# A transformer pair's setup stage: input issued first, parameters on another queue, more slots for the modulation rows, square sums between the turns

## The chip, the cores and the metric

The kernel runs on one core of one Trainium2 chip. The metric is the device time of one execution in microseconds, lower being better: 2711.04 us is the median of 3 runs (2708.45 to 2712.81).

## What is computed

Two transformer blocks in float32 on a sequence of 1024 tokens and 1024 channels. Only the very beginning matters here: a conditioning vector `c` gives six modulation vectors, and the first of them shift and scale the normalised input before the first projection.

```python
def first_block(x, c, w_ada, b_ada, pre_mix_g, w_in, ...):
    c_act = jax.nn.silu(c)
    for l in range(DEPTH):
        mod = c_act @ w_ada[l] + b_ada[l]
        sh1, sc1, g1, sh2, sc2, g2 = [t[:, None, :] for t in jnp.split(mod, N_MOD, axis=-1)]
        h = rms_norm(x, pre_mix_g[l]) * (1.0 + sc1) + sh1
        y = token_mixer(h, w_in[l], ...)
        x = x + g1 * rms_norm(y, post_mix_g[l])
        h = rms_norm(x, pre_ffn_g[l]) * (1.0 + sc2) + sh2
        y = conv_ffn(h, w_up[l], ffn_conv_w[l], ffn_conv_b[l], w_down[l])
        x = x + g2 * rms_norm(y, post_ffn_g[l])
    return x
```

A second block (attention beside a pooling mixer, then a gated feed-forward part) follows; the change does not touch it.

## The kernel before

The activations are kept transposed (128 partitions of channels by 1024 tokens, eight such tiles). Every projection multiplies a weight tile of 1024 by 128, loaded by SyncE (SP) into one of two `raw` buffers, split by ScalarE (`split_hi`, L210) and VectorE (`split_lo`, L215) into a high and a low part, and used by TensorE in three products for each of eight channel tiles and two token halves (`product`, L259). Tile w+2 can be loaded only when tile w has been split (`load`, L197). The kernel is a row of blocks (`nc.Block`), and no engine begins a block before all have ended the one ahead of it.

Block "setup" (L437 to L587), engine by engine, each in its written order:

- GpSimd fills constants (identity, ones, masks). Its first memset, of `par_in`, is what SP waits for.
- SP issues 16 small parameter transfers (L480), `x` in two halves of 2 MB (L484), four rows of the modulation weights `w_ada` (512 KB each, one for each of four slots in `cbuf`, L486), seven very small transfers (L490 to L496), weight tiles 0 and 1 (L204), then twelve more `w_ada` rows, each when its slot has been read, the gate columns (L506), and tiles 2 and 3, which wait until tiles 0 and 1 are split.
- TensorE turns the parameters (L516), then `x`: eight turns of eight 128 by 128 transposes (L523) into two PSUM tiles used in turn; then the sums of squares (`sum_squares`, L368, 16 matmuls of 128x512, each two instructions); then, twice, it sums the accumulator of the modulation rows over the partitions (`reduce_ada`, L374).
- ScalarE makes the sigmoid of `c` (L540), copies the eight turned tiles to `xt` (L543), squares all eight into `squares`, which lies on the space of the input rows `xin` (L547), makes two constants, and splits tiles 0 and 1.
- VectorE copies the parameters (L561), waits for all seven very small transfers and scales the sinks (L563), makes `csil` (L567), adds eight modulation rows (L424, L425), waits for the reduction, makes `mod` (L429), zeroes the gate buffer (L579), adds eight more rows into the same accumulator, waits again, and then splits tiles 0 and 1 (L215) and the gate columns (L586).

Block "w_in" (L745) begins with the normalisation (`Norm.act`, L626: a table load, Ln, Exp, then eight `hhi` tiles; `Norm.dve`, L659: eight scaled tiles and eight `hlo` tiles) on ScalarE and VectorE, and with `pair_products` (L378) on TensorE, which multiplies tiles 0 and 1 as the `hlo` tiles come. Ahead of the normalisation both engines split tiles 2 and 3 (L809 and L905). SP parks `x` in DRAM (L618) and loads two rope tables.

Of the kernel before, what the change touches and what calls it, by code (L numbers as in the profile page):

```python
# [114 lines left out]
def block_kernel(nc, a, out):  # L115
    ctx = ExitStack()
    with ctx:
# [40 lines left out]
        hhi = sb("hhi", [P, DK, T], F32R)  # L158
        hlo = sb("hlo", [P, DK, T], F32R)
# [241 lines left out]
        ada_acc = ar(64, D)  # L401
# [4 lines left out]
        s_par, s_x, s_small = sem("params_loaded"), sem("x_loaded"), sem("small_loaded")  # L406
        s_ada = [sem(f"ada_loaded{i}") for i in range(4)]
# [3 lines left out]
        squares, x_sums = ar(32, DK, T), up[0][:, :]  # L411
# [25 lines left out]
        with nc.Block("setup") as block:  # L437
# [31 lines left out]
            @block.sync  # L469
            def _(sp):  # L470
                sp.wait_ge(s_pool, 1)
                srcs = {"ffn_conv_w01": a["ffn_conv_w"][0, 0:2, :].rearrange("t (j p) -> (t j) p", p=P),
                        "ffn_conv_w2": a["ffn_conv_w"][0, 2:3, :].rearrange("t (j p) -> (t j) p", p=P),
                        "ml_conv_w": a["ml_conv_w"][0].rearrange("t (j p) -> (t j) p", p=P),
                        "ml_norm_g": a["ml_norm_g"][0], "pool_b_2": a["pool_b_2"][0]}
                r = 0
                for name, k in PAR_ROWS:
                    if not name.startswith("pad"):
                        src = srcs[name] if name in srcs else a[name].rearrange("a (j p) -> (a j) p", p=P)
                        sp.dma_start(par_in[r % P:r % P + k, r // P, :], src).then_inc(s_par, 16)  # L480
                    r += k
                xv = a["x"][0].rearrange("(b p) d -> p b d", p=P)
                for b in range(2):
                    sp.dma_start(xin[:, 4 * b:4 * b + 4, :], xv[:, 4 * b:4 * b + 4, :]).then_inc(s_x, 16)  # L484
                def ada_load(slot, seg, k):
                    sp.dma_start(cbuf[:, slot, :], ada_rows(seg, k)).then_inc(s_ada[slot], 16)  # L486

                for k in range(4):
                    ada_load(k, 0, k)
                sp.dma_start(sinks_in, a["attn_sinks"].partition_broadcast(P)[:, 0, :]).then_inc(s_small, 16)  # L490
                for b in range(2):
                    for col, name in ((16, "q_norm_g_2"), (17, "k_norm_g_2")):
                        sp.dma_start(small[64 * b:64 * b + 64, col:col + 1], a[name].rearrange("a p -> p a"))\
                          .then_inc(s_small, 16)
                sp.dma_start(small[0:4, 18:19], a["ml_i_b"].rearrange("a p -> p a")).then_inc(s_small, 16)
                sp.dma_start(small[32:36, 18:19], a["ml_f_b"].rearrange("a p -> p a")).then_inc(s_small, 16)  # L496
                for w in range(RAW):
                    load(sp, At(w), tile_source(At(w)))

                for n in range(4, ADA_FIRST * DK):  # L500
                    sp.wait_ge(ada_added, n - 3)
                    ada_load(n % 4, n // DK, n % DK)
                sp.wait_ge(gate_zero, 1)
                for g in range(2):
                    src = a["w_in"][0].rearrange("(k p) c -> p k c", p=P)[:, :, GATE_COL + 4 * g:GATE_COL + 4 * g + 4]
                    sp.dma_start(gateF[:, :, 32 * g:32 * g + 4], src).then_inc(gate_loaded, 16)  # L506
                for w in range(RAW, 4):
                    load(sp, At(w), tile_source(At(w)))

            @block.tensor  # L510
            def _(pe):
# [6 lines left out]
                pe.wait_ge(s_x, 32)  # L518
                for k in range(DK):
                    if k >= 2:  # L520
                        pe.wait_ge(x_copied, k - 1)
                    for b in range(NB):
                        mm = nc.tensor.transpose(down[k % 2][:, b * P:(b + 1) * P], xin[:, b, k * P:(k + 1) * P],  # L523
                                                 identF[:, :])
                    mm.then_inc(x_turned, 1)

                pe.wait_ge(par_copied, 1)
                for k in range(DK):
                    pe.wait_ge(x_squared, k + 1)
                    sum_squares(x_sums, squares[:, k, :], k == 0, k == DK - 1)  # L530
                for s in range(ADA_FIRST):
                    pe.wait_ge(ada_added, s * DK + DK)
                    reduce_ada(up[1], 0, ada_acc).then_inc(ada_reduced, 1)

            @block.scalar
            def _(act):
                act.sem_inc(hi_done, RAW)
# [3 lines left out]
                for k in range(DK):  # L541
                    act.wait_ge(x_turned, k + 1)
                    nc.scalar.activation(xt[:, k, :], down[k % 2][:, :], ACT.Copy).then_inc(x_copied, 1)  # L543

                for k in range(DK):
                    act.wait_ge(x_copied, k + 1)
                    nc.scalar.activation(squares[:, k, :], xt[:, k, :], ACT.Square).then_inc(x_squared, 1)  # L547
# [3 lines left out]
                nc.scalar.activation(bandR[:, :, :], band, ACT.Copy).then_inc(consts, 1)  # L551
                for w in range(AHEAD):
                    split_hi(act, At(w))
# [4 lines left out]
            def _(dve):  # L558
# [3 lines left out]
                dve.wait_ge(s_small, 16 * 7)  # L562
                nc.vector.tensor_scalar(sinks, sinks_in, 1.0 / SC, None, ALU.mult).then_inc(sinks_scaled, 1)  # L563
# [3 lines left out]
                ch.link(nc.vector.tensor_tensor(csil, csig, par_col("c", 0, 8), ALU.mult))  # L567

                for s in range(ADA_FIRST):
                    for k in range(DK):  # L570
                        dve.wait_ge(s_ada[k % 4], s * 32 + 16 * (k // 4 + 1))
                        if s + k:
                            dve.wait_ge(ada_added, s * DK + k)
                        add_ada_row(ada_acc, cbuf[:, k % 4, :], k).then_inc(ada_added, 1)
                    dve.wait_ge(ada_reduced, s + 1)
                    ch.link(modulate(s, up[1][:, 0:DK]))
                    if s == 0:
                        dve.wait_ge(consts, 3)
                        nc.vector.memset(gateF[:, :, :], 0.0).then_inc(gate_zero, 1)  # L579
# [3 lines left out]
                for w in range(AHEAD):  # L583
                    split_lo(dve, At(w))
# [160 lines left out]
        with nc.Block("w_in") as block:  # L745
# [111 lines left out]
            def _(dve):  # L857
# [46 lines left out]

                for t in range(2):  # L905
                    split_lo(dve, At(t + AHEAD))
                norm_mix.dve(dve)
# [1485 lines left out]
```

## Time and profile before

| what | value |
|---|---|
| median of 3 runs | 2711.04 us (2708.45 to 2712.81) |
| profiled execution, its own time | 2708.46 us |
| its span | 2706.7 us |
| mean granted TensorE clock | 0.957 of full |
| TensorE matmul busy | 2446.0 us (90%) |
| VectorE busy | 1301.5 us (48%) |
| ScalarE busy | 840.2 us (31%) |
| first product matmul of block "w_in" | starts at 83.35 us |

Times in the profile count from the start of the span. A row of a timeline gives start, duration, engine, line, operation, the names it writes and reads, how many instructions are merged, and in brackets the idle time before it and what ended that. A start less the end of the row before it is idle time; a row with x2 holds two instructions back to back.

### The profile page before, as it was taken

Reading aid. Unit: us, or ns where it says so; the run is one execution under the profiler, and the core shown is the slowest. Engines: PE = TensorE matmul, PEld = TensorE weight load, DVE = VectorE, ACT = ScalarE, POOL = GpSimd, SP = SyncE. Lnnn points to the kernel's source line nnn. Section 1 sums busy time; section 2 is a strip of 40 time slices with the busy share of each in tenths; the row PEclk is TensorE's granted clock in tenths of the full one; section 3 lists DMA queues with packets and bytes.
Section 4 is the critical chain, followed back from the end, with each engine's and each line's share of the span. In section 5 each row is a group of like instructions: output and inputs, shape, how many; then the busy total and the mean of one; then the engine's idle time right before and its main releaser. Section 6 shows DMA issues by size and latency. Waiting matters only on the chain. (4 is left out here: it accounts for less than half of the span.)

```text
span 2706.7 us, 28720 instructions
## 1 busy us (share of the span) xinstructions
PE 2446.0 (90%) x10911; PEld 1971.0 (73%) x10911; DVE 1301.5 (48%) x1542; ACT 840.2 (31%) x1200; POOL 275.3 (10%) x206
## 2 busy tenths in 40 slices
PE   4799974569799999999997997898989999999998
PEld 3578864548488888888884865776778888888887
DVE  3467346751744444444446337996343333333333
ACT  3322134642432222222224346875131111111111
POOL 1000011312000000000002424552100000000000
PEclk8899997789899999999998998999999999999999
DMA  5335521002211111111113110002111111111111
GB/s 205 117 109 158 185 72 61 0 24 101 78 47 47 47 46 49 53 53 46 46 46 146 61 32 1 0 0 78 47 39 48 54 46 46 46 46 54 47 46 70
DMA packets 170071, 169.25 MB, mean 63 GB/s; under 512 B 7229, under 2 KB 153485, under 8 KB 169105
## 3 DMA queue, kind: packets, MB, share of 16 engines
q1 hardware_dynamic: 168529, 163.05, 18.6%
q0 software_dynamic: 1472, 5.26, 0.5%
q8 instruction: 45, 0.74, 0.1%
q14 instruction: 25, 0.20, 0.0%
HBM read 146.26 MB, written 22.04 MB: 62 GB/s over the span
## 5 line engine op out<-in xcount | busy, mean ns | idle before, releaser
L267 PE MATMUL ps<-hhi,whi 128*128 128x512 f32 x1984 | 776.2, 391 | 3.4 <-DVE cbuf L1953 2.7
L269 PE MATMUL ps<-hhi,wlo 128*128 128x512 f32 x1984 | 772.0, 389 | 0.0
L268 PE MATMUL ps<-hlo,whi 128*128 128x512 f32 x1984 | 771.9, 389 | 0.0
L215 DVE TENSOR_TENSOR wlo<-raw,whi 128x1024 fp32r<-128x1024 f32 x180 | 231.5, 1289 | 455.0 <-ACT whi L210 454.9
L267 PEld LDWEIGHTS ps<-hhi,whi 128*128 128x128 f32 x1984 | 372.4, 188 | 83.8 <-DVE cbuf L1953 3.1
L268 PEld LDWEIGHTS ps<-hlo,whi 128*128 128x128 f32 x1984 | 372.4, 188 | 78.8 <-issue 1.9
L269 PEld LDWEIGHTS ps<-hhi,wlo 128*128 128x128 f32 x1984 | 372.4, 188 | 77.7
L210 ACT ACTIVATE whi<-raw 128x1024 fp32r<-128x1024 f32 x180 | 186.3, 1049 | 429.4 <-PE ps L1868 299.9
L1985 DVE TENSOR_TENSOR arena<-arena,ps 128x1024 f32<-128x1024 f32 x176 | 214.7, 1220 | 155.6 <-PE ps L1868 154.5
L1866 PE MATMUL ps<-hid_hi,whi 128*128 128x512 f32 x704 | 275.2, 391 | 0.0
L1867 PE MATMUL ps<-hid_lo,whi 128*128 128x512 f32 x704 | 274.1, 389 | 0.0
L1868 PE MATMUL ps<-hid_hi,wlo 128*128 128x512 f32 x704 | 273.9, 389 | 0.0
L1493 POOL TENSOR_TENSOR cbuf<-cbuf,attn_stats 128x1024 f32<-128x1024 f32 x80 | 151.5, 1894 | 216.1 <-DVE attn_stats L1619 216.1
L1949 DVE SCALAR_TENSOR_TENSOR cbuf<-ps,par,cbuf 128x1023 f32<-128x1023 f32 x44 | 56.4, 1283 | 235.7 <-ACT cbuf L1893 235.6
L1866 PEld LDWEIGHTS ps<-hid_hi,whi 128*128 128x128 f32 x704 | 132.1, 188 | 31.4 <-DVE arena L1985 4.1
L1868 PEld LDWEIGHTS ps<-hid_hi,wlo 128*128 128x128 f32 x704 | 132.1, 188 | 27.7
L1867 PEld LDWEIGHTS ps<-hid_lo,whi 128*128 128x128 f32 x704 | 132.1, 188 | 27.1
L1749 POOL TENSOR_TENSOR cbuf<-cbuf 128x1024 f32<-128x1024 f32 x18 | 43.1, 2394 | 936.8 <-ACT cbuf L1739 936.8
L1893 ACT ACTIVATE cbuf<-ps,par 128x1024 f32<-128x1024 f32 x44 | 53.1, 1206 | 240.9 <-PE ps L269 232.3
L392 PE MATMUL ps<-hhi,whi 128*128 128x512 f32 x192 | 80.7, 420 | 45.8 <-DVE hlo L690 23.5
L1539 PE MATMUL ps<-identF,cbuf 128*128 128x128 f32 x640 | 93.9, 292 | 21.0 <-POOL cbuf L1493 15.7
L1907 ACT ACTIVATE hid_hi<-cbuf 128x1024 fp32r<-128x1024 f32 x44 | 46.5, 1058 | 211.0 <-DVEq L1964 115.6
(277 smaller groups left out, 2704.4 us busy)
## 6 DMA issues: line engine op xcount, KB each, us to landing
raw<-in_w_up SPq DMA_DIRECT2D x66, 512.0 KB, 3.6
raw<-in_w_down SPq DMA_DIRECT2D x44, 512.0 KB, 3.5
raw<-in_w_in SPq DMA_DIRECT2D x32, 512.0 KB, 5.9
arena<-in_w_ada SPq DMA_DIRECT2D x32, 512.0 KB, 5.1
x_park<-arena SPq DMA_DIRECT2D x3, 4096.0 KB, 12.3
raw<-in_w_gate SPq DMA_DIRECT2D x22, 512.0 KB, 3.6
cbuf<-in_w_ada SPq DMA_DIRECT2D x16, 512.0 KB, 5.3
raw<-in_w_out SPq DMA_DIRECT2D x16, 512.0 KB, 3.3
```

The source lines that it names most:

```text
L210: nc.scalar.activation(whi[:, w.off % RING, :], raw[:, w.off % RAW, :], ACT.Copy).then_inc(hi_done, 1)
L215: nc.vector.tensor_tensor(wlo[:, w.off % RING, :], raw[:, w.off % RAW, :], whi[:, w.off % RING, :].bitcast(F32), ALU.subtract).then_inc(lo ...
L267: nc.tensor.matmul(acc[:, tok], whi[:, s, ws], hhi[:, k, tok], start=(k == 0), stop=False)
L268: nc.tensor.matmul(acc[:, tok], whi[:, s, ws], hlo[:, k, tok], start=False, stop=False)
L269: mm = nc.tensor.matmul(acc[:, tok], wlo[:, s, ws], hhi[:, k, tok], start=False, stop=(k == DK - 1))
L392: nc.tensor.matmul(o, whi[:, s, ws], hhi[:, k, tok], start=(k == 0), stop=False)
L1493: nc.gpsimd.tensor_tensor(p, p, st[:, sl, 16:16 + q].unsqueeze(2).to_broadcast([P, q, T // q]), ALU.mult).then_inc(S["scaled"], 1)
L1539: mm = nc.tensor.transpose(ps_t[:, (4 * h + k) * P:(4 * h + k + 1) * P], src, identF[:, :])
L1866: nc.tensor.matmul(o, whi[:, s, ws], hidhi[:, p, tok], start=(r == 0), stop=False)
L1867: nc.tensor.matmul(o, whi[:, s, ws], hidlo[:, p, tok], start=False, stop=False)
L1868: mm = nc.tensor.matmul(o, wlo[:, s, ws], hidhi[:, p, tok], start=False, stop=(r == 1))
L1985: nc.vector.tensor_tensor(y[:, fo, :], y[:, fo, :], down[fo % 2][:, :], ALU.add)\
```

## The change

In SP's program `x` comes first and no longer waits for GpSimd; then eleven `w_ada` rows at once (four slots in `cbuf`, seven in `chunk_work`, which is the space of `hhi`), tiles 0 and 1, the gate columns, the last five `w_ada` rows, tiles 2 and 3. The 16 parameter transfers and the seven very small ones are issued by ScalarE. TensorE takes a sum of squares between two turns, starts a turn of the first half of `x` before the second is there, and reduces the first accumulator after the fifth sum. The second set of rows has its own accumulator and its own PSUM columns. ScalarE squares each tile right after its copy, into `lead_work` (the space of `hlo`). VectorE no longer waits for the small transfers before `csil`, zeroes the gate buffer first, adds all 16 rows with one `mod` step after the thirteenth, and splits tiles 0 and 1 before the second `mod` step. In block "w_in" the normalisation comes ahead of the splits of tiles 2 and 3.

```diff
@@ block "setup", SP
-                sp.wait_ge(s_pool, 1)
+                xv = a["x"][0].rearrange("(b p) d -> p b d", p=P)
+                for b in range(2):
+                    sp.dma_start(xin[:, 4 * b:4 * b + 4, :], xv[:, 4 * b:4 * b + 4, :]).then_inc(s_x[b], 16)
+                for n in range(len(ada_slots)):
+                    ada_load(n)
+                for w in range(RAW):
+                    load(sp, At(w), tile_source(At(w)))
+                sp.wait_ge(gate_zero, 1)
+                for g in range(2):
...
+                    sp.dma_start(gateF[:, :, 32 * g:32 * g + 4], src).then_inc(gate_loaded, 16)
+                for n in range(len(ada_slots), ADA_FIRST * DK):
+                    sp.wait_ge(ada_added, n - len(ada_slots) + 1)
+                    ada_load(n)
+                for w in range(RAW, 4):
+                    load(sp, At(w), tile_source(At(w)))
@@ block "setup", TensorE
+                turn(0)
+                turn(1)
+                pe.wait_ge(par_copied, 1)
+                for k in range(DK):
+                    if k + 2 < DK:
+                        turn(k + 2)
+                    sums(k)
+                    if k == 4:
+                        pe.wait_ge(ada_added, DK)
+                        reduce_ada(up[1], 0, ada_acc[0]).then_inc(ada_reduced, 1)
+                pe.wait_ge(ada_added, 2 * DK)
+                reduce_ada(up[1], HALF, ada_acc[1]).then_inc(ada_reduced, 1)
@@ block "setup", ScalarE
+                act.wait_ge(s_pool, 1)
...
+                        act.dma_start(par_in[r % P:r % P + k, r // P, :], src).then_inc(s_par, 16)
                 nc.scalar.activation(csig, par_col("c", 0, 8), ACT.Sigmoid).then_inc(c_sig, 1)
                 nc.scalar.activation(identR[:, :], identF[:, :], ACT.Copy).then_inc(consts, 1)
                 nc.scalar.activation(bandR[:, :, :], band, ACT.Copy).then_inc(consts, 1)
+                act.dma_start(sinks_in, a["attn_sinks"].partition_broadcast(P)[:, 0, :]).then_inc(s_small, 16)
...
+                for k in range(DK):
+                    act.wait_ge(x_turned, k + 1)
+                    nc.scalar.activation(xt[:, k, :], down[k % 2][:, :], ACT.Copy).then_inc(x_copied, 1)
+                    act.wait_ge(x_copied, k + 1)
+                    nc.scalar.activation(squares[:, k, :], xt[:, k, :], ACT.Square).then_inc(x_squared, 1)
@@ block "setup", VectorE
-                dve.wait_ge(s_small, 16 * 7)
-                nc.vector.tensor_scalar(sinks, sinks_in, 1.0 / SC, None, ALU.mult).then_inc(sinks_scaled, 1)
+                dve.wait_ge(consts, 3)
+                nc.vector.memset(gateF[:, :, :], 0.0).then_inc(gate_zero, 1)
+                for n in range(ADA_FIRST * DK):
+                    slot, k = n % len(ada_slots), n % DK
+                    dve.wait_ge(s_ada[slot], 16 * (n // len(ada_slots) + 1))
...
+                    if n == 12:
+                        dve.wait_ge(ada_reduced, 1)
+                        ch.link(modulate(0, up[1][:, 0:DK]))
+                for w in range(AHEAD):
+                    split_lo(dve, At(w))
+                dve.wait_ge(ada_reduced, 2)
+                ch.link(modulate(1, up[1][:, HALF:HALF + DK]))
@@ block "w_in", ScalarE (VectorE likewise)
+                norm_mix.act(act)
                 for t in range(2):
                     split_hi(act, At(t + AHEAD))
-                norm_mix.act(act)
```

## Rows read from the trace of the kernel before

**Rows 1.** The page: busy time, share of the span and instructions of each engine.
```profile
PE 2446.0 (90%) x10911; PEld 1971.0 (73%) x10911; DVE 1301.5 (48%) x1542; ACT 840.2 (31%) x1200; POOL 275.3 (10%) x206
```

**Rows 2.** Timeline of TensorE (start, duration, line, idle and releaser), first 84 us.
```profile
8.51 0.87 PE L516 MATMUL ps<-identF,arena 128*128 128x128 f32 x3 [8.51 <-DMA arena<-in_ffn_conv_b]
19.82 11.03 PE L523 MATMUL ps<-identF,arena 128*128 128x128 f32 x64 [10.44 <-DMA arena<-in_x]
33.00 15.47 PE L368 MATMUL ps<-arena,onesF 128*128 128x512 f32 x32 [2.15 <-ACT arena L547]
48.31 1.84 PE L374 MATMUL ps<-onesF,arena 128*128 128x1 f32 x16
...
62.49 3.57 PE L374 MATMUL ps<-onesF,arena 128*128 128x1 f32 x16 [12.35 <-DVE arena L425]
83.35 0.77 PE L392 MATMUL ps<-hhi,whi 128*128 128x512 f32 x1 [17.29 <-DVE hlo L690]
```

**Rows 3.** Timeline of VectorE, first 80 us.
```profile
26.33 0.17 DVE L563 TENSOR_SCALAR small<-small 128x8 f32<-128x8 f32 x1 [16.35 <-DMA small<-in_ml_f_b]
...
27.48 5.45 DVE L425 SCALAR_TENSOR_TENSOR arena<-cbuf,small,arena 128x1024 f32<-128x1024 f32 x4
...
66.10 0.17 DVE L429 TENSOR_TENSOR mod<-ps,par 128x8 f32<-128x8 f32 x1 [3.66 <-PE ps L374]
...
66.46 2.35 DVE L215 TENSOR_TENSOR wlo<-raw,whi 128x1024 fp32r<-128x1024 f32 x2
68.73 0.68 DVE L586 TENSOR_TENSOR gateR<-gateF,gateR 128x512 fp32r<-128x512 f32 x1
...
79.42 2.48 DVE L679 SCALAR_TENSOR_TENSOR cbuf<-arena,coef,cbuf 128x1024 f32<-128x1024 f32 x2 [2.29 <-ACT cbuf L624]
```

**Rows 4.** Timeline of ScalarE, first 77 us.
```profile
21.83 1.02 ACT L543 ACTIVATE arena<-ps 128x1024 f32<-128x1024 f32 x1 [11.61 <-PE ps L523]
23.54 1.02 ACT L543 ACTIVATE arena<-ps 128x1024 f32<-128x1024 f32 x1 [0.68 <-PE ps L523]
...
26.46 2.02 ACT L543 ACTIVATE arena<-ps 128x1024 f32<-128x1024 f32 x2 [0.19 <-PE ps L523]
...
31.81 7.67 ACT L547 ACTIVATE arena<-arena 128x1024 f32<-128x1024 f32 x8
...
74.82 1.06 ACT L210 ACTIVATE whi<-raw 128x1024 fp32r<-128x1024 f32 x1 [2.44 <-DMA raw<-in_w_in]
75.89 1.28 ACT L628 ACT_TABLE_LOAD   x1
```

**Rows 5.** Timeline of SP's queue: the issues of transfers, first 70 us.
```profile
1.19 0.40 SPq L480 DMA_DIRECT2D arena<-in_b_ada  x1
...
7.23 0.96 SPq L484 DMA_DIRECT2D arena<-in_x  x2
...
10.27 1.24 SPq L490 DMA_DIRECT2D small<-in_attn_sinks  x1
...
16.58 5.30 SPq L204 DMA_DIRECT2D raw<-in_w_in  x2
...
69.69 0.34 SPq L618 DMA_DIRECT2D x_park<-arena  x1
```

**Rows 6.** Stretches: us, five engines' busy time, then granted TensorE clock, DMA share, GB/s.
```profile
10.00:20.00 10.00, 0.18 (x1) 0.18 (x2) 0.00 (x0) 0.21 (x1) 0.00 (x0) 1.00 1.02 415
...
30.00:40.00 10.00, 7.85 (x21) 3.83 (x20) 6.58 (x6) 9.80 (x12) 0.00 (x0) 0.83 0.94 316
...
60.00:70.00 10.00, 3.57 (x16) 3.48 (x16) 5.61 (x8) 0.63 (x1) 0.00 (x0) 0.50 0.21 38
```

**Rows 7.** The same view in stretches of 1 us: the clock around the sums of squares.
```profile
32.00:33.00 1.00, 0.00 (x0) 0.03 (x1) 0.94 (x1) 1.00 (x2) 0.00 (x0) 0.80 1.01 332
...
35.00:36.00 1.00, 1.00 (x3) 0.48 (x2) 0.88 (x2) 1.00 (x2) 0.00 (x0) 0.50 1.06 422
36.00:37.00 1.00, 1.00 (x3) 0.41 (x3) 0.90 (x2) 1.00 (x2) 0.00 (x0) 0.99 1.03 401
```

**Rows 8.** Transfers issued in the first 110 us: how many, size, median time to landing.
```profile
gateF<-in_w_in SPq DMA_DIRECT2D x2, 16.0 KB, 5.0
```

More of the change, by code:

```diff
@@ L158, in block_kernel @@
         hhi = sb("hhi", [P, DK, T], F32R)
+        with nc.sbuf_tensor("lead_work", [P, DK * T], F32) as lead_work:
+            pass
         hlo = sb("hlo", [P, DK, T], F32R)
@@ L400, in block_kernel @@
         xin = ar(32, NB, D)
-        ada_acc = ar(64, D)
+        ada_acc = [ar(64, D), chunk_work[:, 7 * D:8 * D]]
+        ada_slots = [cbuf[:, i, :] for i in range(4)] + [chunk_work[:, i * D:(i + 1) * D] for i in range(7)]
         par_in = ar(68, 3, P)
@@ L470, in _ @@
             def _(sp):
-                sp.wait_ge(s_pool, 1)
[L472 to L481, printed above, removed]
@@ L517, in _, with turn @@
                 mm.then_inc(par_turned, 1)
-                pe.wait_ge(s_x, 32)
-                for k in range(DK):
+                def turn(k):
                     if k >= 2:
@@ L522, in _ @@
                     for b in range(NB):
+                        if k == 0 and b % 4 == 0:
+                            pe.wait_ge(s_x[b // 4], 16)
                         mm = nc.tensor.transpose(down[k % 2][:, b * P:(b + 1) * P], xin[:, b, k * P:(k + 1) * P],
@@ L525, in _, with sums @@
                     mm.then_inc(x_turned, 1)
+                def sums(k):
+                    pe.wait_ge(x_squared, k + 1)
+                    sum_squares(x_sums, squares[:, k, :], k == 0, k == DK - 1)
+                turn(0)
+                turn(1)
                 pe.wait_ge(par_copied, 1)
                 for k in range(DK):
[L529 to L533, printed above, removed]
+                    if k + 2 < DK:
[6 more added lines that the diff above has]
+                reduce_ada(up[1], HALF, ada_acc[1]).then_inc(ada_reduced, 1)
             @block.scalar
             def _(act):
+                act.wait_ge(s_pool, 1)
+                srcs = {"ffn_conv_w01": a["ffn_conv_w"][0, 0:2, :].rearrange("t (j p) -> (t j) p", p=P),
+                        "ffn_conv_w2": a["ffn_conv_w"][0, 2:3, :].rearrange("t (j p) -> (t j) p", p=P),
+                        "ml_conv_w": a["ml_conv_w"][0].rearrange("t (j p) -> (t j) p", p=P),
+                        "ml_norm_g": a["ml_norm_g"][0], "pool_b_2": a["pool_b_2"][0]}
+                r = 0
+                for name, k in PAR_ROWS:
+                    if not name.startswith("pad"):
+                        src = srcs[name] if name in srcs else a[name].rearrange("a (j p) -> (a j) p", p=P)
+                        act.dma_start(par_in[r % P:r % P + k, r // P, :], src).then_inc(s_par, 16)
+                    r += k
                 act.sem_inc(hi_done, RAW)
@@ L582, in _ @@
                                                 ALU.mult))
-                for w in range(AHEAD):
-                    split_lo(dve, At(w))
+                dve.wait_ge(s_small, 16 * 7)
+                nc.vector.tensor_scalar(sinks, sinks_in, 1.0 / SC, None, ALU.mult).then_inc(sinks_scaled, 1)
                 dve.wait_ge(gate_hi, 1)
```

52 lines of the change are left out of this document (16 added, 36 removed).

## The prediction

> **What bounds the kernel now.** I read the page's busy line first, then the timelines of TensorE, VectorE, ScalarE and SP over the first 84 us, then the table of stretches for clock and transfers. TensorE is busy 2446.0 of 2706.7 us [rows 1]: almost the whole kernel is paced by its products, so an edit of the setup is worth what it moves the first product, now at 83.35 us, and nothing else. Behind that point the order of work is the same in both kernels.
>
> TensorE's timeline shows four holes ahead of 83.35: until 19.82 it waits for `x`, for 2.15 us before the sums, 12.35 us before the second reduction, and 17.29 us before the first product [rows 2]. Each has its cause on another engine. `x` is issued only at 7.23, behind 16 parameter transfers that begin at 1.19 [rows 5]. VectorE stands still until 26.33, waiting for the last very small transfer, before it may add a modulation row [rows 3]; these went through SP's queue behind `x` and four rows [rows 5]. The first reduction is queued behind all sums and starts at 48.31 [rows 2], and the second eight rows wait for it, since they share the accumulator. In the last hole VectorE splits tiles 0 and 1 (2.35 us) [rows 3], only then can tiles 2 and 3 be loaded, and ScalarE waits for tile 3 until 74.82 before it starts the normalisation with a table load at 75.89 [rows 4].
>
> **The change part by part.** I rebuild the time line of the setup.
>
> Input. From the issue at 7.23 to the first turn at 19.82 are 12.6 us for both halves [rows 2, 5]. Without the wait for GpSimd the issue can begin at about 0.7, so both halves are in at 13.3; the first half may be turned earlier, which gives nothing, as will be seen.
>
> Parameters on ScalarE. SP needed (7.23 - 1.19) / 16 = 0.38 us for each issue [rows 5]. ScalarE starts at 1.2 to 2.2 (its table load may come first) and ends at 7.2 to 8.2. The trace has no transfer on a second hardware queue, so their landing is bounded: some 1.5 us after the last issue, as SP's last parameter issue just ahead of 7.23 and the turn at 8.51 show [rows 2, 5], gives 8.9; served only after `x`, 13.3; served after `x` and eleven rows (below), 27. I take 11, between the first two, since the source names only 336 rows of 512 bytes, beside 4 MB. From the parameter turn to `csil` are some 1.7 us, so VectorE can add rows from about 13.5, against 26.4 before.
>
> Small transfers on ScalarE. What they now hold up is ScalarE itself: the seven issues took from 10.27 to 16.58, 6.3 us, on SP [rows 5], and behind them in ScalarE's order stand the copies of `x`. With the sigmoid at 12.7 and two constants (0.9) the copies begin at 13.6 + 6.3 = 19.9. At 0.38 us each they would begin at 16.3; I keep 6.3, the same transfers' own price beside other traffic. So `x` arriving at 13.3 is not what ends last.
>
> Turns, squares and sums. ScalarE needs a copy and a square for each tile, 1.02 + 7.67 / 8 = 1.98 us [rows 4]. TensorE needs a turn and a sum. A turn takes 1.70 us at the pace of the first ones (23.54 - 21.83) [rows 4] and half, 0.85, at the other level of the clock. The sums took 15.47 us with the clock at 0.50 until 36, 3 us [rows 2, 7]; without that half lost it is 15.47 - 1.5 = 13.97, or 1.75 each. So TensorE at 2.60 a tile, not ScalarE, sets the pace. From the first copy: 1.1 for it, six turns 5.1 (two are done), the sums 13.97, the first reduction 1.84 [rows 2], and 2.0 for about 4 us at half clock at the start: 24.0. That ends at 43.9, against 50.15 before; the eight copies and squares are hidden under it.
>
> Modulation rows. A row of 524 KB at 415 GB/s takes 1.26 us, at the 316 GB/s of the mixed stretch 1.66 [rows 6]. After `x` at 13.3 eleven rows take 13.9 to 18.2; I take 14.3, as the ten pure microseconds show. Tiles 0 and 1 in 512-byte pieces: at least 3.3 at 316 GB/s, at most 5.3 (the time SP was held by them) [rows 5]; 4.5. Gate columns: 0 to 5.0 [rows 8]; 2. The last five rows, 1.4 each: 7. One more for the landing: 42.1, and the last add (5.45 / 4 = 1.36) [rows 3] ends at 43.5. VectorE alone would need 0.75 + 15 x 1.36 = 21 us from 13.5, so transfers bound it. Bounds of this chain: 41 to 51.
>
> End of the setup. The second reduction starts at 43.9 and takes 1.84, or 3.57 if the clock has fallen (0.50 around the one at 62.49) [rows 2, 6]; the splits of tiles 0 and 1 lie beside it. Then `mod`, gains, sinks and the gate split (0.68) [rows 3]: 1.3, and 0.3 to the next block: 47.4, against 69.7 (SP parks `x` at 69.69) [rows 5]. That saves 22.3.
>
> Normalisation ahead of the splits. Before, table load to first product took 83.35 - 75.89 = 7.5 us, from a block start of 69.7: 6.2 us of waiting and splitting go. Now 47.4 + 0.2 + 7.5 = 55.1. The splits of tiles 2 and 3 (2.1 on ScalarE, 2.5 on VectorE) fall after the normalisation, some 17 us after the first product, under the pair products and the gate products; the third tile is wanted some 34 us after it. Loads 4 and 5 follow them and keep over 10 us of cover. If that cover were gone, up to 5 us would come back. ScalarE also waits there for the parked `x`; its 4 MB should need about as long as those of `x`, 12.6 us, and the normalisation ends later than that.
>
> Sum: 83.35 - 55.1 = 28.2 us. The profiled execution took 2708.46 us, so it would take 2680.2; the median of the runs is 2.6 higher, at 2711.04, and the forecast for the median is 2682.8, rounded to 2683.
>
> A rule of the Trainium skill stands against the second queue: "DMA: Bandwidth & Descriptors", section "Issuing engines are not separate DMA queues", says that another issuing engine saves the issue time alone. By the section "Queues, rings and completion order" of the same page a DMA engine takes turns between its queues, which would land the parameters early, near 9 us; no row of this trace has two such queues.
>
> **The rivals.**
>
> *The second queue is held up (price: 10 to 20 us of the gain).* SP was held 5.30 us for two tile loads and 1.24 for a single small transfer while `x` and four rows were on their way [rows 5], so issuing stalls when much is outstanding. Now 13 large transfers go out at once. If ScalarE's issues stall along with SP's, the parameters land at 20 to 27, the copies begin 9 to 16 us later, TensorE's 24 us follow, and the time is 2692 to 2699. For: those stalls. Against: they are seen on one queue only, and the two issues of `x` took 0.96 us together.
>
> *The clock stays at 1.2 GHz through the mixed stream.* Turns cost 1.70 and sums 3.4; six turns, eight sums, and reductions of 3.57 from 19.9 + 1.1 end at 62; the second reduction and the rest bring the block's end to 67, the first product to 75, and the time to 2702. In this trace the clock dropped between 32 and 33 (0.80) [rows 7], some 2 us after the turns ended, but the turns themselves doubled their pace from 1.70 to 1.1 (two copies in 2.2) [rows 4], and the sums reached 0.99 after 3 us. Half of this rival, low clock in parts, gives 2690. The page "TensorE: Matmul & The Clock Gate", section "Part 4: PE-mode transpose", says that transposes do not count as busy for the clock; the doubled pace of the turns speaks against it here.
>
> *Slower than before: ScalarE as the issuer.* The mechanism is the first rival at both places: the parameters wait for SP's whole backlog, about 33 us, and the seven small issues then stall beside the gate columns and late rows at over twice their 6.3 us, 16. Copies begin at 33 + 2.6 + 16 = 52, TensorE ends at 76, the first product comes at 87 and the time is 2715. It decides when the copies begin later than about 48.
>
> *It does not do what it says.* If the normalisation's first product still waited for something behind the block's start (the parked `x` or the tiles), only the 22 us remain: 2689.
>
> **How the numbers follow.** Forecast case, with the ends of its bounds (2676 with early parameters and small issues at 0.38, 2689 with slow rows and low clock at the last reduction): 0.66. Queue held up, 2689 to 2699: 0.18. Low clock, 2690 to 2702: 0.08. Only 22 us: 0.05. Slower: 0.02, and 0.01 for a gain within 5.4 us. The range 2677 to 2697 leaves out the worst of the queue and clock cases and the very best. About 0.2% (5.4 us) is what a measurement of this kernel can tell from no change: faster by more 0.95, within 0.03, slower 0.02.
>
> **What would show it.** The first product at 55 (50 to 62). Parameter turn at about 11; later than 14 speaks for the queue rival. First copy of `x` at 20, last sum near 44, clock at 1 from about 27. Last modulation add at 43 to 44 with transfers as its releaser. The parking of `x` issued at 47 to 48, the table load right behind it. The same length from first product to end as before, 2706.7 - 83.35 = 2623 us; a difference there, such as a wait for tile 2 or 4, would make the sum wrong.

## The result and the profile after

The changed kernel takes 2679.4 us, the median of 4 runs (2679.14 to 2684.59), against 2709.74 us for the kernel before, also the median of 4 runs: ratio 0.9891, 95% interval 0.9874 to 0.9908. The forecast was 2683.0, with a range of 2677 to 2697. The profiled execution took 2679.24 us with a span of 2677.4, 29.3 us shorter than before.

TensorE's timeline up to the first product (as [rows 2]: start, duration, line, idle and releaser):

```profile
14.78 0.87 PE L503 MATMUL ps<-identF,arena 128*128 128x128 f32 x3 [14.78 <-DMA arena<-in_ffn_conv_b]
15.44 3.13 PE L512 MATMUL ps<-identF,arena 128*128 128x128 f32 x16
21.35 1.94 PE L512 MATMUL ps<-identF,arena 128*128 128x128 f32 x8 [2.77 <-ACT arena L563]
23.08 2.72 PE L370 MATMUL ps<-lead_work,onesF 128*128 128x512 f32 x4
25.64 1.04 PE L512 MATMUL ps<-identF,arena 128*128 128x128 f32 x8
26.51 1.88 PE L370 MATMUL ps<-lead_work,onesF 128*128 128x512 f32 x4
...
36.01 1.84 PE L376 MATMUL ps<-onesF,arena 128*128 128x1 f32 x16
37.71 1.07 PE L512 MATMUL ps<-identF,arena 128*128 128x128 f32 x8
38.62 5.32 PE L370 MATMUL ps<-lead_work,onesF 128*128 128x512 f32 x12
43.77 1.84 PE L376 MATMUL ps<-onesF,chunk_work 128*128 128x1 f32 x16
54.51 0.77 PE L394 MATMUL ps<-hhi,whi 128*128 128x512 f32 x1 [8.90 <-DVE hlo L706]
```

The first product starts at 54.51 instead of 83.35: 28.84 us earlier. From there to the end the kernel takes 2677.4 - 54.51 = 2622.89 us, before it was 2623.35. So the whole gain lies ahead of the first product: in the setup and in the first steps of block "w_in". The holes of 12.35 and 2.15 us [rows 2] are gone; from 21.35 to 45.6 TensorE works without a stop, one turn (eight transposes) and one sum at a time (start to start 2.6 us). The last hole shrank from 17.29 to 8.90.

ScalarE's timeline and the queue it issues on (ACTq rows are issues of transfers):

```profile
7.50 0.40 ACTq L544 DMA_DIRECT2D arena<-in_ffn_conv_b  x1
16.28 0.21 ACT L549 ACTIVATE small<-par 128x8 f32<-128x8 f32 x1 [6.92 <-DVE par L575]
16.40 0.36 ACTq L554 DMA_DIRECT2D small<-in_attn_sinks  x1
...
19.82 0.31 ACTq L560 DMA_DIRECT2D small<-in_ml_f_b  x1
20.18 1.02 ACT L563 ACTIVATE arena<-ps 128x1024 f32<-128x1024 f32 x1 [2.97 <-issue]
21.23 1.06 ACT L565 ACTIVATE lead_work<-arena 128x1024 f32<-128x1024 f32 x1
...
47.05 1.28 ACT L644 ACT_TABLE_LOAD   x1 [3.70 <-PEq L441]
```

Two things are to be seen. The last parameter transfer is issued at 7.50 and the parameters are turned only at 14.78. And before its first copy ScalarE is idle for 2.97 us with "issue" as the cause: it is handing out the seven small transfers. The table load starts with the block, at 47.05 (75.89 before [rows 4]).

VectorE and SP, the stretches that matter:

```profile
17.85 0.63 DVE L428 TENSOR_SCALAR arena<-cbuf,small 128x1024 f32<-128x1024 f32 x1
...
35.58 1.28 DVE L429 SCALAR_TENSOR_TENSOR chunk_work<-cbuf,small,chunk_work 128x1024 f32<-128x1024 f32 x1 [3.92 <-DMA cbuf<-in_w_ada]
...
41.80 1.28 DVE L429 SCALAR_TENSOR_TENSOR chunk_work<-chunk_work,small 128x1024 f32<-128x1024 f32 x1
```

```profile
0.75 0.99 SPq L477 DMA_DIRECT2D arena<-in_x  x2
...
4.05 10.23 SPq L481 DMA_DIRECT2D chunk_work<-in_w_ada  x7
14.39 11.03 SPq L206 DMA_DIRECT2D raw<-in_w_in  x2
25.47 5.09 SPq L490 DMA_DIRECT2D gateF<-in_w_in  x2
...
47.04 0.34 SPq L634 DMA_DIRECT2D x_park<-arena  x1
```

VectorE adds rows from 17.85 (26.62 before) and the last row is added at 43.08. SP is held for 10.23 and 11.03 us in its issues, where the two issues of `x` took 0.99: the transfers, which kept the DMA engines busy (share about 1.0 from 14 to 20 us), and not their requests, set that pace.

### The profile page after: what moved, and what is told of

Same layout as the page of the kernel before. It is cut to its first block and busy times, and to the rows that moved or that the text cites. A ratio compares the mean times of both kernels' runs of the same rounds, so it can differ in the third digit from the quotient of the medians.

```text
span 2677.4 us, 28725 instructions
## 1 busy us (share of the span) xinstructions
PE 2441.1 (91%) x10911; PEld 1968.3 (74%) x10911; DVE 1301.3 (49%) x1542; ACT 840.6 (31%) x1200; POOL 275.3 (10%) x206
```

## The experiments

Each row is one profiled execution; only the kernel before, the changed one and the last two were also timed in 4 runs or more. What I read is where the first product starts (F) and how long the rest takes (R, span less F). In the changed kernel F is 54.51 and R 2622.9. R turned out to have two values; the last section shows most of the reason, and so F, and not the span, tells what an edit of the setup does. But F is moved by TensorE's clock too: the first sum of squares took 2.72 us in the changed kernel and 3.62 in three kernels with the same program on TensorE and ScalarE up to there (splits first, gate columns late, four slots), whose second reduction started 1.1 to 1.5 us later. A difference of F under some 1.5 us says nothing about an edit until the rows are read. One caution for the clock column: it can read 1.00 early in a profile while the pace is that of half clock (in the kernel before from 20 to 25 us, with turns 1.70 us apart). There the pace tells the level.

| kernel | span | F | R |
|---|---|---|---|
| before | 2706.7 | 83.35 | 2623.4 |
| changed | 2677.4 | 54.51 | 2622.9 |
| before, normalisation first | 2698.3 | 75.35 | 2623.0 |
| changed, splits first | 2687.0 | 59.46 | 2627.5 |
| small transfers late | 2682.4 | 54.68 | 2627.7 |
| gate columns late | 2683.6 | 56.03 | 2627.6 |
| both late | 2674.8 | 51.66 | 2623.1 |
| parameters on SP | 2690.8 | 61.84 | 2629.0 |
| `x` in pieces of 1 KB | 2680.1 | 55.11 | 2625.0 |
| sums after turns | 2681.7 | 59.04 | 2622.7 |
| four slots | 2683.2 | 55.61 | 2627.6 |
| one accumulator | 2688.3 | 60.49 | 2627.8 |
| root in the setup | 2671.6 | 48.44 | 2623.2 |
| and small matmuls apart | 2670.7 | 48.24 | 2622.5 |

### The order of normalisation and splits

In the kernel before:

```diff
-                for t in range(2):
-                    split_hi(act, At(t + AHEAD))
                 norm_mix.act(act)
+                for t in range(2):
+                    split_hi(act, At(t + AHEAD))
```

(and the same for `split_lo` on VectorE).

> The kernel before with one edit: the normalisation ahead of the splits of tiles 2 and 3. My theory: the setup still ends near 69.7 us, the table load follows at once (about 69.9 instead of 75.89), and the first product starts at 77.4 instead of 83.35, 6 us earlier; the span falls by 6, to about 2700.7. Rival: the normalisation waits for something else at the block's start (the parking of x, tiles on their way), and the first product stays above 80.

F came to 75.35, 8.0 us earlier. ScalarE and SP both start the block at 67.89, against 69.69 [rows 5]:

```profile
67.89 1.28 ACT L628 ACT_TABLE_LOAD   x1 [7.10 <-PEq L437]
```

From table load to first product are 7.46 us, exactly as before (83.35 - 75.89). The order is worth 75.89 - 69.69 = 6.2 us as expected. The other 1.8 us lie in the setup, which this edit does not touch:

```profile
32.66 13.97 PE L368 MATMUL ps<-arena,onesF 128*128 128x512 f32 x32 [2.15 <-ACT arena L547]
```

The sums took 13.97 us instead of 15.47 [rows 2], which is 1.5 of the 1.8 us: here the clock did not fall ahead of them. 13.97 is the figure that the prediction had worked out for the full clock.

The same edit undone in the changed kernel:

```diff
+                for t in range(2):
+                    split_hi(act, At(t + AHEAD))
                 norm_mix.act(act)
-                for t in range(2):
-                    split_hi(act, At(t + AHEAD))
```

> The changed kernel with one edit undone: the splits of tiles 2 and 3 stand ahead of the normalisation again. Theory: tiles 2 and 3 are requested at 44.3 and 44.7 us there, before the block ends at 47, land some 4 us later and are split by about 51, so the table load starts near 51.3 instead of 47.05 and the first product at 58.5 instead of 54.51, 4 us later. Rival: the order is worth the full 6.2 us as in the kernel before, first product at 60.7.

F 59.46, 4.95 later. The block started at 48.46 (47.04), since the first sum ran at the pace of half clock for longer (3.62 us against 2.72), though the clock column reads 1.00 there:

```profile
23.24 3.62 PE L370 MATMUL ps<-lead_work,onesF 128*128 128x512 f32 x4
24.00:25.00 1.00, 1.00 (x3) 0.39 (x2) 0.90 (x2) 1.00 (x2) 0.00 (x0) 1.00 1.04 402
```

The table load came at 52.00. So the order itself costs 52.00 - 48.46 = 3.5 us here, near the 4 expected and less than 6.2, because tiles 2 and 3 are requested 3.7 us ahead of the block's start (44.78) and not 1.9 (67.75, with the block at 69.69).

### Which chain ends the setup

Small transfers on SP behind the last rows:

```diff
@@ ScalarE
-                act.dma_start(sinks_in, ...).then_inc(s_small, 16)
...
@@ SP, behind the last rows
+                sp.dma_start(sinks_in, ...).then_inc(s_small, 16)
...
```

> The changed kernel with the seven very small transfers moved from ScalarE to SP, behind the last modulation rows. Theory: they cost ScalarE 3.7 us ahead of its first copy of x, so the copy starts near 17.3 instead of 20.18 and TensorE reaches the second reduction 2.9 us earlier, at 40.9; but the last row is added only at 43.08, so the reduction starts at about 43.2 and the first product at 53.9, only 0.6 earlier. Rival: the rows' chain is not next in line, and the first product moves the full 2.9, to 51.6.

F 54.68, nothing gained. TensorE shows the reason:

```profile
15.58 4.70 PE L519 MATMUL ps<-identF,arena 128*128 128x128 f32 x24
20.12 1.88 PE L370 MATMUL ps<-lead_work,onesF 128*128 128x512 f32 x4
...
34.82 5.32 PE L370 MATMUL ps<-lead_work,onesF 128*128 128x512 f32 x12
42.76 3.04 PE L376 MATMUL ps<-onesF,chunk_work 128*128 128x1 f32 x16 [2.63 <-DVE chunk_work L429]
```

The first copy came at 17.53 and the sums ended 3.8 us earlier, at 40.1; then TensorE waited 2.63 us for the last row, and the reduction took 3.04 instead of 1.84, with the clock at 0.69 from 43 to 44 us and 0.50 behind that. Without these 1.2 us F would have been about 53.5 (an estimate), near the 53.9 expected.

Gate columns behind the last rows:

```diff
-                sp.wait_ge(gate_zero, 1)
-                ...  # two gate transfers
                 for n in range(len(ada_slots), ADA_FIRST * DK):
                     sp.wait_ge(ada_added, n - len(ada_slots) + 1)
                     ada_load(n)
+                sp.wait_ge(gate_zero, 1)
+                ...  # two gate transfers
```

> The changed kernel with the gate columns requested behind the last five modulation rows instead of ahead of them. Theory: SP was held 5.09 us by the two gate transfers and VectorE stood still for 3.92 us at 31.6; the last row is now added at about 39 instead of 43.08, but TensorE's own chain (turns, sums, first reduction) still ends at 43.77, so the first product stays at 54.5. Rival: the rows were what bounded, and the first product comes 2 to 4 us earlier.

F 56.03, 1.5 later and not earlier. The longer half clock in the first sum (3.62 us against 2.72) and in the turns around it explains that: the second reduction started at 45.30. The last row was added at 43.67, not at 39 as I had said, and VectorE names a wait that I had overlooked:

```profile
39.42 0.17 DVE L433 TENSOR_TENSOR mod<-ps,par 128x8 f32<-128x8 f32 x1 [3.85 <-PE ps L376]
```

The `mod` step after the thirteenth row waits for the first reduction, and three rows stand behind it.

Both together:

> The changed kernel with both edits: small transfers on SP behind everything and gate columns behind the last rows. Theory: two chains of nearly the same length end the setup, TensorE's (second reduction at 43.77) and the modulation rows' (last add at 43.08); with both shortened the second reduction starts near 40.9 and the first product at 51.6, 2.9 us earlier, although either edit alone gives under 1 us. Rival: the two edits add nothing together, first product above 53.5.

F 51.66, 2.85 earlier, as expected. Two chains of nearly the same length end the setup, and either edit alone gains nothing that shows (0.2 and 1.5 us later, with 1.2 and 1.5 us of half clock in them). TensorE still waits for the last row, but 1.10 us only:

```profile
40.67 1.95 PE L376 MATMUL ps<-onesF,chunk_work 128*128 128x1 f32 x16 [1.10 <-DVE chunk_work L429]
```

### The second queue

Parameters back on SP ahead of `x`:

```diff
@@ SP
+                sp.wait_ge(s_pool, 1)
+                ...  # the 16 parameter transfers
                 xv = a["x"][0].rearrange("(b p) d -> p b d", p=P)
```

> The changed kernel with the 16 parameter transfers back on SP ahead of x, the rest as changed. Theory: the parameters land at 8.5 instead of 14.8, but x and all modulation rows come 6.5 us later: x at 19.8, the first copy at 21.8 (20.18 before the edit), the last row added at about 49.6 instead of 43.08, the first product at 60.5 to 61, 6 us later. Rival: since the parameters hold up csil and TensorE in the changed kernel, bringing them early makes up for the later x, and the first product moves by no more than 2 us.

F 61.84, 7.3 later. The parameters were turned at 8.67, but `x` was issued at 7.24 instead of 0.75, the first copy came at 22.48 and TensorE waited for the last row until 50.12, 6.35 us later than its start at 43.77. The other 1.0 us is the reduction, 2.83 us instead of 1.84, at a clock of 0.50 from 51 us. The transfers bound this kernel, and the issue order on SP is worth more than early parameters.

`x` in pieces of 1 KB:

```diff
-                    sp.dma_start(xin[:, 4 * b:4 * b + 4, :], xv[:, 4 * b:4 * b + 4, :]).then_inc(s_x[b], 16)
+                    for h in range(4):
+                        sp.dma_start(xin[:, 4 * b:4 * b + 4, 256 * h:256 * h + 256],
+                                     xv[:, 4 * b:4 * b + 4, 256 * h:256 * h + 256]).then_inc(s_x[b], 16)
...
```

> The changed kernel with x loaded by eight transfers of 1 KB pieces instead of two of 4 KB pieces, same bytes. In the changed kernel the last parameter transfer is issued at 7.5 and the parameters are turned only at 14.78. Theory: each small piece of the parameters waits for one large piece of x on its DMA engine, so with pieces a quarter of the size the parameters are there at 9.5 to 11. Rival: they wait for the bytes of x as a whole, and are turned at 14 to 15 again. The first product should move by under 1 us either way, since the last modulation row bounds it.

Neither. The parameters were turned at 13.21, 1.6 us earlier, while the second half of `x` landed later:

```profile
13.21 0.87 PE L505 MATMUL ps<-identF,arena 128*128 128x128 f32 x3 [13.21 <-DMA arena<-in_ffn_conv_b]
...
15.62 2.82 PE L514 MATMUL ps<-identF,arena 128*128 128x128 f32 x12 [0.69 <-DMA arena<-in_x]
```

So the parameters do not wait for all of `x`, and the size of its pieces explains little of the 7 us; F moved by 0.6. The edit is not a clean test, since it also held SP for 7.81 us in the issues of `x` (0.99 before it) and so put fewer bytes on their way early. The last section shows what the 7 us consist of; their cause stays open.

### Interleaving, slots, accumulators

All turns, then all sums; all copies, then all squares:

```diff
+                for k in range(2, DK):
+                    turn(k)
                 for k in range(DK):
-                    if k + 2 < DK:
-                        turn(k + 2)
                     sums(k)
@@ ScalarE
                     nc.scalar.activation(xt[:, k, :], down[k % 2][:, :], ACT.Copy).then_inc(x_copied, 1)
+                for k in range(DK):
                     act.wait_ge(x_copied, k + 1)
```

> The changed kernel with the interleaving undone: all turns, then all sums on TensorE; all copies, then all squares on ScalarE. Theory: turns 2 to 7 then run at ScalarE's pace (6.6 us and more at low clock), the sums start at about 31, take 15.5, the two reductions 3.7, and the setup's last reduction ends near 50.2 instead of 45.61; first product at 59, 4.5 us later. Rival: the order is worth nothing, because TensorE has the same work to do, and the first product stays within 1 us of 54.5.

F 59.04, 4.5 later, as expected:

```profile
26.92 2.01 PE L512 MATMUL ps<-identF,arena 128*128 128x128 f32 x16 [0.24 <-ACT arena L563]
30.99 10.55 PE L370 MATMUL ps<-lead_work,onesF 128*128 128x512 f32 x20 [2.06 <-ACT lead_work L566]
```

The sums took 15.6 us (30.99 to 41.37 and 43.07 to 48.31). This order costs clock too: behind the 2.06 us of waiting it read 0.50 from 33 to 35 us.

Four slots instead of eleven:

```diff
-        ada_slots = [cbuf[:, i, :] for i in range(4)] + [chunk_work[:, i * D:(i + 1) * D] for i in range(7)]
+        ada_slots = [cbuf[:, i, :] for i in range(4)]
```

> The changed kernel with four slots for the modulation rows instead of eleven. Theory: rows 4 to 15 are then requested only as VectorE frees a slot, from 18.6 us on, and behind tiles 0 and 1; each takes 3 to 5 us to land with up to four under way, so the last row is added at 44 to 46 instead of 43.08 and the first product comes at 56 to 58, 1.5 to 3 us later than 54.51. Rival: the slots are the main gain of the setup, and the first product goes beyond 62.

F 55.61, 1.1 later, less than my lower bound. The last row was added at 44.54, but TensorE's sums, slowed again by a first sum of 3.62 us, ended later still (reduction at 44.88, with no wait). So in this profile the 1.1 us are the clock's; with the sums at the changed kernel's pace the four slots would cost about 44.54 - 43.77 = 0.8 us (an estimate). The seven more slots are hidden almost wholly behind the other chain; row by row VectorE waited 3.02 us once, otherwise 1.4 or less.

One accumulator:

```diff
-        ada_acc = [ar(64, D), chunk_work[:, 7 * D:8 * D]]
+        ada_acc = [ar(64, D), ar(64, D)]
...
-                    if n == 12:
+                    if n == 7:
                         dve.wait_ge(ada_reduced, 1)
```

> The changed kernel with one accumulator for both modulation vectors: the ninth row may be added only when the first reduction has been read. Theory: TensorE makes the first reduction after the fifth sum, at 36.0 to 37.8 (or up to 39.3 where the clock rises later), and only then the eight rows of the second half, 10.2 us, can be added, so the last one is done at 48.5 to 50 instead of 43.08, the second reduction ends at 50.3 to 53, and the first product comes at 59.5 to 62, 5 to 7 us later. Rival: the wait is hidden, since the last rows land only at 40; first product within 1 us of 54.5.

F 60.49, 6.0 later: the second reduction started 4.9 us later (48.65) and took 2.96 us instead of 1.84, with the clock lower behind TensorE's wait of 4.69 us. The wait that the second accumulator removes comes back:

```profile
37.91 0.17 DVE L433 TENSOR_TENSOR mod<-ps,par 128x8 f32<-128x8 f32 x1 [9.81 <-PE ps L376]
```

### A faster version

Both transfers late, the first `mod` step behind the last row, and the root of the first normalisation in the setup:

```diff
@@ setup, ScalarE, at its end
+                nc.scalar.preload_act_table_set("natural_log_exp_and_others")
+                act.wait_ge(ada_added, len(ada_slots))
+                act.wait_ge(x_summed, 1)
+                nc.scalar.activation(cbuf[:, 2, :], x_sums, ACT.Ln, bias=eps, scale=1.0 / D).then_inc(sem("norm_mix_logs"), 1)
+                act.wait_ge(sem("norm_mix_logs"), 1)
+                nc.scalar.activation(cbuf[:, 2, :], cbuf[:, 2, :], ACT.Exp, scale=-0.5).then_inc(sem("norm_mix_rstd"), 1)
@@ Norm.act
-                nc.scalar.preload_act_table_set(LN_EXP)
+                early = self.name == "norm_mix"
+                if not early:
+                    nc.scalar.preload_act_table_set(LN_EXP)
...
-                self.act_rstd(act, last)
+                if not early:
+                    self.act_rstd(act, last)
...
```

> A version that should beat the changed kernel: small transfers and gate columns late as in the run with both edits, the first mod step behind the last row, and the table load, Ln and Exp of the first normalisation on ScalarE inside the setup, under the last row and the second reduction (the late slots are exchanged so that cbuf is free). Theory: the block w_in starts at 44.2 as in the run with both edits, and VectorE begins at once, so the first product comes near 48.2 instead of 51.66, and the time is about 2673 where the clock holds near 155 us and 2677 where it drops there. Rival: Ln waits for the last sum and becomes the new end of the setup, and the first product stays above 50.

F 48.44. In 4 runs it took 2673.31 us (2671.71 to 2677.4) beside 2708.25 for the kernel before; ratio 0.9875, interval 0.9858 to 0.9891. Against the changed kernel it was not timed side by side, and the interval overlaps that of the changed kernel (0.9874 to 0.9908), so the times alone do not show it to be faster; the profiles do, with the first product 6.1 us earlier at an R within 0.3. ScalarE's three steps lie under the last row, the splits and the second reduction, and VectorE starts the block at once:

```profile
40.45 1.28 ACT L573 ACT_TABLE_LOAD   x1
41.74 1.11 ACT L576 ACTIVATE cbuf<-ps,small 128x1024 f32<-128x1024 f32 x1
42.88 1.06 ACT L578 ACTIVATE cbuf<-cbuf 128x1024 f32<-128x1024 f32 x1
```

```profile
44.51 2.48 DVE L706 SCALAR_TENSOR_TENSOR cbuf<-arena,coef,cbuf 128x1024 f32<-128x1024 f32 x2 [0.33 <-PEq L442]
```

The last kernel adds an edit in block "w_in", for the clock (last section):

```diff
+                    if t == 7:
                         for h in range(ML_H):
                             mm = nc.tensor.matmul(gates_out[:, P + h * NB:P + (h + 1) * NB], selF[:, h, :],
...
@@ VectorE
-                    if t == 7:
+                    if t == 8:
                         dve.wait_ge(g_pe, 1)
```

> As the version with the root in the setup, with one more edit in block w_in: the 4x8 matmuls with selF come after the product of the eighth tile instead of right behind the 32 gate transposes of 4 columns, so 3.6 us of very small matmuls in one stretch become 2.1 and 1.5 apart. Theory: in five of eight runs so far (clock at 0.5 for some 4 to 7 us just behind this stretch, near 155 to 167 us, at 3 to 5 us of cost) the clock fell because of it; apart, it should stay at 1.00 there in every run, and all runs should lie within 1.5 us of each other. Rival: the drop has another cause, and single runs still lie 4 to 5 us above the others.

2673.42 us in 4 runs (2672.45 to 2674.32), ratio 0.9873, interval 0.9857 to 0.989: no faster in the median. The spread is 1.9 us against 5.7 without the edit, a little over the 1.5 expected, and no run lies 4 us above the others.

## Why the prediction was right, and where its terms were off

The forecast of 2683 stood on the first product at 55.1 and nothing behind it; measured were 54.51 and R equal within 0.5 us. For the profiled execution the sum gave 2680.2, measured 2679.24. Most of the rest between 2683 and 2679.4 is the 2.6 us by which the median of the first three runs stood above their profiled execution; I carried it over, and after the change the difference is 0.2.

The way there was right in its main steps: `x` no longer waits, the copies wait for the small transfers, TensorE's mixed stream and the rows' transfers end close together, and nothing behind the first product changes. Part of the close hit is luck, in two places: two terms ahead of the first copy were off by 3.8 and 2.6 us in opposite directions, and the clock rose early in the changed kernel's profile. In the three profiles with a first sum of 3.62 us the way from the first copy to the second reduction took 24.8 us, 1.2 more than here.

- *Input first.* Issued at 0.75 (said 0.7). Its landing was hidden, as said: TensorE turned it at 15.44 without a wait, and ScalarE's first copy waits for something else.
- *Parameters.* Said 11, measured 14.78, outside the two bounds I had chosen between (8.9 and 13.3), though inside the widest (27). This was the worst term, and by the prediction's own sign (later than 14) it speaks for the queue rival. The other queue's issues did not stall, 16 in 6.7 us from 1.19, so of that rival the stall was wrong and the late landing partly right. The reading that turn-taking between queues would land them near 9 did not come either. VectorE added rows from 17.85 and not from 13.5, partly because its zeroing of the gate buffer waited for ScalarE's constants until 17.45; TensorE's chain hid this.
- *Small transfers.* Said 6.3 us, measured 3.7 (16.40 to 20.13), nearer to the other end (2.7 at 0.38 us each). The parameters came 3.8 us too late; 2.6 us came back here, and 0.8 because the issues ran beside the two constants, which the sum had put ahead of them. So the first copy, at 19.9 said, was measured at 20.18.
- *Turns, squares, sums.* Said 24.0 us from the first copy to the second reduction, measured 43.77 - 20.18 = 23.6. The pace of 2.60 us a tile was measured as 2.59, and TensorE, not ScalarE, set it. Of the 2.0 us for half clock at the start 1.7 came: the turn at 21.35 and the sum at 23.08 took 4.29 us together. The undone order cost 4.5 us.
- *Rows.* Last add said 43.5, measured 43.08, held up by transfers once for 3.92 us and once for 0.69. Right in its sum, but the wait of the `mod` step for the first reduction was missing from it; it stayed hidden in the changed kernel and showed with the gate columns late.
- *End of the setup and normalisation first.* Block start 47.4 said, 47.04 measured; 7.46 us from table load to first product in both. The saving of 6.2 us was confirmed by the edit alone in the kernel before.
- *Clock.* The rival of a clock held low through the mixed stream did not come: it read 1.00 from 25 us to the end of the setup. The prediction called the turns' change from 1.70 to 1.1 us a doubled pace; the 1.1 was ScalarE's pace of copying (two copies in 2.2 us). In the kernel with small transfers late three turns alone (24 transposes, 4.70 us), back to back behind the turn of the parameters, were followed by a first sum of 1.88 us, the pace of the high level. The sentence of the Trainium skill that transposes do not count as busy ("TensorE: Matmul & The Clock Gate", "Part 4: PE-mode transpose") does not hold for these float32 turns.
- *Chances.* The cases add up to 0.01 for a gain within 5.4 us, where the last line has 0.03 for a change within it; nothing else hangs on it.
- *Slower side and "does not do what it says".* Neither came; `x_park` and the late splits stayed under the products.

Of the parts, measured one by one in the changed kernel: parameters off SP's queue 7.3 us, two accumulators 6.0 (each with 1.0 to 1.1 us of a slower reduction in it), interleaving 4.5, normalisation first 3.5 (6.2 in the kernel before), eleven slots 1.1 at most. They do not add up to 28.8 one by one, since each is measured with the others in place and two chains of nearly equal length hide parts of each other. One part was not undone in any run: that VectorE no longer waits for the seven small transfers before it adds rows (26.62 before, 17.85 after). Its worth alone is not shown.

## What to carry to other kernels

Rebuild the time line of a setup from rows, engine by engine, and look for the second-longest chain: with two chains of 43.77 and 43.08 us neither edit alone gave anything, both together 2.9 us. Look at what stands ahead of the large transfers in the order of issue: 16 small ones ahead of `x` cost 7.3 us here. Don't hand out small transfers from an engine that is about to start the chain: seven of them held ScalarE's first copy back by 2.7 to 2.9 us. A step whose inputs are ready early, here the root of a normalisation, belongs ahead of the block boundary (first product at 48.44 instead of 51.66).

## What the hardware showed that I had not expected

**A clock that falls while TensorE is busy.** R is 2622.5 to 2623.4 in seven of the fourteen profiles and 2627.5 to 2629.0 in six (2625.0 in one). In those six and the one at 2625.0 the granted clock is 0.50 for 3 to 7 us near 155 to 168 us; in the seven shorter ones it stays at 1.00 there. In the kernel with small transfers late (us, five engines' busy time, clock, DMA share, GB/s):

```profile
155.00:156.00 1.00, 1.00 (x16) 1.00 (x15) 1.00 (x1) 0.00 (x0) 0.00 (x0) 1.00 0.00 0
156.00:157.00 1.00, 1.00 (x7) 0.98 (x6) 0.96 (x2) 0.00 (x0) 0.00 (x0) 0.51 0.00 0
```

```profile
153.57 2.13 PE L811 MATMUL ps<-identF,arena 4*128 4x4 f32 x32
155.56 1.45 PE L814 MATMUL ps<-arena,selF 4*128 4x8 f32 x8
...
157.53 0.63 PE L270 MATMUL ps<-hlo,whi 128*128 128x512 f32 x1
```

TensorE shows as fully busy, but what it does are 40 matmuls of 4 and 8 columns on 4 rows; behind them the big products take 0.63 instead of 0.39 us. The same stretch in the changed kernel's profile (L811 at 152.74) passed without a fall. The price can be read from the start of these matmuls to the next reduction, first in the changed kernel, then in the one with small transfers late:

```profile
152.74 2.13 PE L811 MATMUL ps<-identF,arena 4*128 4x4 f32 x32
210.24 1.84 PE L376 MATMUL ps<-onesF,arena 128*128 128x1 f32 x16
214.25 1.84 PE L376 MATMUL ps<-onesF,arena 128*128 128x1 f32 x16
```

That is 57.5 us without a fall (the same in all six profiles that have none and keep this order) and 60.7 with one. So a fall costs 3.2 us in five profiles, and 1.6 in two where it is half as long (parameters on SP, `x` in pieces), and not the 3 to 5 us of the last expectation. The rest of the gap in R lies elsewhere: 0.5 to 0.9 us in the first products behind F, which run at half clock for longer in the six profiles (until about 60.4 instead of 58.5 in the one with small transfers late), and what remains further on, which I did not follow. Single runs of one kernel differ by as much, 2684.59 among three of 2679.1 to 2679.6, with a mean granted clock of 0.959 against 0.961 and 0.962; that this run had such a fall is likely but not shown, since no profile of it was read. With the two groups of small matmuls starting 13 us apart the clock read 1.00 from 140 to 180 us and the spread fell to 1.9 us in 4 runs. That the small matmuls cause the fall and the edit prevents it is likely; but the stretch in its old order passed without a fall in six of the other 13 profiles, so one profile and 4 runs don't settle it.

**A small transfer on a second queue beside a full first one.** The last of the 16 parameter transfers took 7 us from issue to use in the changed kernel, about 1.5 before, with `x` and the rows moving on the other queue. The small queue is q10 (packets, MB, share of 16 engines); first the changed kernel from 0 to 5 us and from 5 to 14, then the one with `x` in pieces of 1 KB from 3 to 13:

```profile
q1 hardware_dynamic: 241, 0.99, 57.0%
q1 hardware_dynamic: 880, 3.47, 95.9%
q10 hardware_dynamic: 478, 0.17, 7.3%
q1 hardware_dynamic: 3356, 3.33, 95.8%
q10 hardware_dynamic: 481, 0.17, 7.0%
```

Up to 5 us no packet of the small queue had moved, although its first transfer was issued at 1.19. From then on it was served beside the full one, some 50 packets a microsecond, until just before the turn at 14.78. That agrees with the Trainium skill ("DMA: Bandwidth & Descriptors", "Queues, rings and completion order") that a DMA engine takes turns between its queues, but at a price of microseconds. With pieces of a quarter of the size the small queue moved at about the same rate and only began earlier. So the late landing is a late beginning and then a slow run of many small packets; why the queue began so late, and what sets its rate, no run here shows.
